# Norm joints: squares ahead of scaled copies, sums of squares inside the dense stream, and products into an unread bank

## The reference

```
block 1, layer l:  u = rms_norm(h, g);  p = u @ w_in            (projection)
                   three mixers (rwkv7, hgrn2, sparse attention) and their gates
                   h = h + (sum of gate * branch) @ w_o          (merge)
                   u = rms_norm(h, g);  h = h + conv_glu(u)      (FFN, width 2816)
                   after layer 1: h = rms_norm(h, g)             (final norm)
block 2, layer l:  h = h + 0.5 * swiglu(rms_norm(h, g))          (FFN)
                   u = rms_norm(h, g);  projection, three mixers, merge
                   h = h + 0.5 * swiglu(rms_norm(h, g))          (FFN)
                   after layer 1: final norm
rms_norm(x, g) = x * rsqrt(mean(x * x over the width) + 1e-6) * g
```

## Time and profile before

| | |
|---|---|
| median of 3 runs | 3233.77 us (3233.0 to 3235.81) |
| the profiled execution | 3229.9 us |
| its span, first to last instruction | 3228.1 us |
| TensorE matmul busy | 2859.5 us, 89% |
| TensorE weight load busy | 2452.1 us, 76% |
| VectorE busy | 1922.0 us, 60% |
| ScalarE busy | 1361.9 us, 42% |
| mean granted TensorE clock | 0.915 of full |

### The profile page before, as it was taken

The page is one execution under the profiler, slowest core; times in us unless marked ns, Lnnn a source line. Parts: engine busy times, 40 slices in busy tenths (PEclk is TensorE's granted clock), DMA queues, the critical chain, the costliest instruction groups (busy, mean ns, idle before and its releaser), DMA issues. The chain is left out here.

```text
span 3228.1 us, 53616 instructions
## 1 busy us (share of the span) xinstructions
PE 2859.5 (89%) x23052; PEld 2452.1 (76%) x23052; DVE 1922.0 (60%) x2576; ACT 1361.9 (42%) x1873; POOL 151.7 (5%) x116
## 2 busy tenths in 40 slices
PE   7898678999897778999998998889999989988899
PEld 6787557888786657888886875678888878756688
DVE  5754766965655766956555444666565644446564
ACT  5413334645413244645453232545454532325443
POOL 0030000000030000000000310000000012000000
PEclk9998888998898888998998998989999988989899
DMA  5211114564111123555542111245645411203453
GB/s 213 92 40 53 66 54 148 197 212 157 66 43 63 66 81 137 202 187 183 198 144 74 40 66 40 93 143 202 220 170 197 141 64 40 72 34 119 138 201 131
DMA packets 54667, 386.18 MB, mean 120 GB/s; under 512 B 6688, under 2 KB 7328, under 8 KB 8352
## 3 DMA queue, kind: packets, MB, share of 16 engines
q1 hardware_dynamic: 54432, 382.76, 34.5%
HBM read 381.69 MB, written 1.05 MB: 119 GB/s over the span
## 5 line engine op out<-in xcount | busy, mean ns | idle before, releaser
L320 PE MATMUL banks<-normed_high,weights_high 128*128 128x256 f16 (+1 forms) x4096 | 1150.7, 281 | 49.6 <-DVE normed_low L414 22.6
L321 PE MATMUL banks<-normed_low,weights_high 128*128 128x256 f16 (+1 forms) x4096 | 1149.7, 281 | 0.0
L322 PE MATMUL banks<-normed_high,weights_low 128*128 128x256 f16 (+1 forms) x4096 | 1148.1, 280 | 0.0
L306 DVE SCALAR_TENSOR_TENSOR weights_low<-weight_ring,weights_high 128x2048 f16<-128x2048 f32 x334 | 761.1, 2279 | 417.2 <-ACT weights_high L300 402.8
L300 ACT ACTIVATE weights_high<-weight_ring 128x2048 f16<-128x2048 f32 x306 | 580.2, 1898 | 299.3 <-PE banks L322 284.0
L320 PE MATMUL banks<-projected,weights_high 128*128 128x256 f16 x1696 | 471.7, 278 | 73.3 <-DVE projected L331 73.3
L320 PEld LDWEIGHTS banks<-normed_high,weights_high 128*128 128x128 f16 (+1 forms) x4096 | 412.8, 101 | 126.3 <-issue 47.3
L321 PE MATMUL banks<-projected,weights_high 128*128 128x256 f16 x1696 | 471.8, 278 | 0.0
L322 PE MATMUL banks<-projected,weights_low 128*128 128x256 f16 x1696 | 471.3, 278 | 0.0
L322 PEld LDWEIGHTS banks<-normed_high,weights_low 128*128 128x128 f16 (+1 forms) x4096 | 411.9, 101 | 59.6
L321 PEld LDWEIGHTS banks<-normed_low,weights_high 128*128 128x128 f16 (+1 forms) x4096 | 411.3, 100 | 59.2 <-issue 1.8
(11 more groups left out here) (390 smaller groups left out, 3251.8 us busy)
## 6 DMA issues: line engine op xcount, KB each, us to landing
weight_ring<-w SPq DMA_DIRECT2D x356, 1024.0 KB, 4.9
small_weights<-small SPq DMA_DIRECT2D x2, 1280.0 KB, 7.9
constants<-const SPq DMA_DIRECT2D x1, 1601.0 KB, 10.1
weight_ring<-w SPq DMA_DIRECT2D x2, 640.0 KB, 3.8
residual<-xt SPq DMA_DIRECT2D x1, 1024.0 KB, 5.0
small_weights<-small SPq DMA_DIRECT2D x2, 512.0 KB, 10.4
out<-residual SPq DMA_DIRECT2D x4, 256.0 KB, 2.8
parameters<-par SPq DMA_DIRECT2D x2, 115.5 KB, 9.6
```

Source lines behind the costliest of these rows:

```text
L306: nc.vector.scalar_tensor_tensor(out=self.part(self.mem.w_low, g), in0=self.part(self.mem.ring, g), scalar=W_SCALE, in1=self.part(self.mem ...
L320: pe.matmul(out, w_high, high, start=start, stop=False, skip_group_check=skip)
L321: pe.matmul(out, w_high, low, start=False, stop=False, skip_group_check=skip)
L322: return pe.matmul(out, w_low, high, start=False, stop=stop, skip_group_check=skip)
```

## The change

- `before_root` gets the next stage's first two weight copies. For an FFN behind a merge (`spaced`) the list is now: table load, squares 0, scaled 0, weight copy, squares 1, scaled 1, weight copy, squares 2, scaled 2, squares 3, root, scaled 3. Elsewhere: table load, both weight copies, squares 0, scaled 0, squares 1, scaled 1, squares 2, squares 3, scaled 2, root, scaled 3.
- The sums are cut into blocks (`sum_two`). In a merge, block 0 stands ahead of tile j=2, block 1 ahead of j=3, block 2 in the middle of j=3. In the last down job block 0 stands ahead of output tile 6. What is not moved stays in `sum`.
- `keep_clock` issues float16 matmuls, 256 columns of a constant tile, into a bank that nobody reads: eight ahead of the last block of sums, four behind it, eight behind the spread.
- `normed`, high and low work in five pieces (1, 1, 2, 2, 2 tiles) instead of four blocks; in the final norms `normed` stays in blocks of two tiles.
- In the FFN stage the low part of the next stage's second job moves from behind residual block 0 to behind block 3.
- In the middle of the program the FFN behind the final norm, and the final norms themselves, use the second order of ScalarE's list. The final norm's TensorE part is as in any norm.

```diff
+def keep_clock(pe, mem, bank, count):
+    still = mem.c("ident").bitcast(F16)
+    for _ in range(count):
+        pe.matmul(mem.ps[:, bank, 0:T], still[:, 0:P], still, start=True, stop=True)
...
+    PIECES = ((0, 1), (1, 1), (2, 2), (4, 2), (6, 2))
...
-    def before_root(self, act, nc):
+    def before_root(self, act, nc, highs, spaced):
+
         nc.scalar.activation(self.unread, self.mem.c("eps", 1), ACT.Sqrt)
+        if not spaced:
+            for high in highs:
+                high(act)
         for b in range(3):
             self.squares(act, nc, b)
-            self.gained(act, nc, b)
+            if b < 2 or spaced:
+                self.gained(act, nc, b)
+            if b < 2 and spaced:
+                highs[b](act)
         self.squares(act, nc, 3)
+        if not spaced:
+            self.gained(act, nc, 2)
         self.root(act, nc)
         self.gained(act, nc, 3)
...
+    def sum_two(self, pe, b):
+
+        assert b == self.summed
+        self.summed += 1
+        pe.wait_ge(self.sig("squares"), b + 1)
+        for k in (2 * b, 2 * b + 1):
             for n in range(NBLK):
                 mm = pe.matmul(self.mem.ps[:, self.sums + n, 0:2], self.u[:, k, n * P:(n + 1) * P],
-                               self.mem.c("ones", 2), start=(k == 0), stop=(k == KT - 1))
-        mm.then_inc(self.sig("square_sums"), 1)
+                               self.mem.c("ones", 2), start=(k == 0), stop=(k == KT - 1),
+                               skip_group_check=True)
+        if b == 3:
+            mm.then_inc(self.sig("square_sums"), 1)
+
+    def sum(self, pe):
+        for b in range(self.summed, 4):
+            if b == 3:
+                keep_clock(pe, self.mem, self.idle_bank, 8)
+            self.sum_two(pe, b)
+        keep_clock(pe, self.mem, self.idle_bank, 4)
 
     def spread(self, pe):
...
         mm.then_inc(self.sig("spread"), 1)
+        keep_clock(pe, self.mem, self.idle_bank, 8)
...
     def scale(self, dve, nc):
+
         self.inverse(dve, nc)
         dve.wait_ge(self.sig("spread"), 1)
-        for b in range(4):
-            self.normed(dve, nc, b, self.u)
-            if b:
-                self.low(dve, nc, b - 1)
-        self.low(dve, nc, 3)
+        last = len(self.PIECES) - 1
+        self.normed(dve, nc, *self.PIECES[0], self.u)
+        for i in range(last):
+            self.normed(dve, nc, *self.PIECES[i + 1], self.u)
+            self.low(dve, nc, i)
+        self.low(dve, nc, last)
...
@@ merge_stage, tensor
             pe.wait_ge(sig("lows"), 6 + j + 1)
+            if j >= 2:
+                following.sum_two(pe, j - 2)
             for n in range(2):
+                if (j, n) == (3, 1):
+                    following.sum_two(pe, 2)
...
@@ ffn_stage, vector
-        next_low(dve, 0)
+        following.low(dve, 0)
...
-            if b == 0:
-                next_low(dve, 1)
+        following.low(dve, 1)
...
@@ ffn_stage, tensor
             for o in range(KT):
+                if i == DOWN - 1 and o == KT - 2:
+                    following.sum_two(pe, 0)
...
-        LOW_SPARE, HIGH_SPARE = (2, 2), (4, 4)
+        LOW_SPARE, HIGH_SPARE = (2, 2, 1), (4, 4, 6)
```

More of the change, by code:

```diff
@@ L341, with __init__ @@
 class Norm:
-    def __init__(self, mem, cut, sig, gain, ready, sums, spread):
+    PIECES = ((0, 1), (1, 1), (2, 2), (4, 2), (6, 2))
+    def __init__(self, mem, cut, sig, gain, ready, sums, spread, idle):
         self.mem, self.sig, self.ready = mem, sig, ready
         self.gain, self.sums, self.spread_bank = CG[gain], sums, spread
+        self.idle_bank, self.summed = idle, 0
         self.u, self.scaled = cut(KT, T), cut(KT, T)
@@ L404, in inverse, with normed, low @@
         nc.vector.reciprocal(self.stat, self.stat).then_inc(self.sig("inverse"), 1)
[L406 to L409, removed]
+    def normed(self, dve, nc, k, n, out):
+        dve.wait_ge(self.sig("gained"), k // 2 + 1)
+        inverse = self.mem.ps[:, self.spread_bank, 0:T].unsqueeze(1).to_broadcast([P, n, T])
+        nc.vector.tensor_tensor(out[:, k:k + n, :], self.scaled[:, k:k + n, :], inverse, ALU.mult
                                 ).then_inc(self.sig("normed"), 1)
[L412 to L416, removed]
+    def low(self, dve, nc, i):
+        k, n = self.PIECES[i]
+        dve.wait_ge(self.sig("u_high"), i + 1)
+        nc.vector.scalar_tensor_tensor(out=flat(self.mem.u_low[:, k:k + n, :]),
+                                       in0=flat(self.u[:, k:k + n, :]), scalar=X_SCALE,
+                                       in1=flat(self.mem.u_high[:, k:k + n, :]), op0=ALU.mult,
                                        op1=ALU.subtract).then_inc(self.sig("u_low"), 1)
@@ L465, in scalar @@
         link, say, need = linker(act, sig, "act_ops")
-        for g in jobs[:2]:
-            stream.high(act, nc, sig, g)
-        norm.before_root(act, nc)
+        norm.before_root(act, nc, [lambda act, g=g: stream.high(act, nc, sig, g)
+                                   for g in jobs[:2]], False)
         norm.highs(act, nc)
@@ L646, in end, with merge_stage @@
         self.out(act, nc, sig, 2 * len(self.jobs) - 1)
-def merge_stage(nc, mem, sig, stream, first, bias, next_low):
+def merge_stage(nc, mem, sig, stream, first, bias, following):
     y_pair = mem.proj[:, 0:3 * MT_, :].bitcast(F16)
@@ L768, in merge_stage, with ffn_stage @@
     return Part(sync, scalar, vector, tensor)
-def ffn_stage(nc, mem, sig, stream, first, gain, ready, spare, conv, factor, loads, next_low):
+def ffn_stage(nc, mem, sig, stream, first, gain, ready, spare, conv, factor, loads, following,
+              spaced=True):
     cut = Cutter(mem.scratch)
@@ L942, in tensor, with final_norm_stage @@
                 mm.then_inc(sig("tiles_done"), 1)
-    return Part(sync, scalar, vector, tensor), early_low, loaded
-def final_norm_stage(nc, mem, sig, gain, ready, spare, next_low, store=None):
+    return Part(sync, scalar, vector, tensor), Early(early_low, norm.sum_two)
+def final_norm_stage(nc, mem, sig, gain, ready, spare, following, store=None):
     norm = Norm(mem, Cutter(mem.scratch), sig, gain, ready, *spare)
@@ L966, in vector @@
         for b in range(4):
-            norm.normed(dve, nc, b, mem.h)
+            norm.normed(dve, nc, 2 * b, 2, mem.h)
             if b % 2:
-                next_low(dve, b // 2)
+                following.low(dve, b // 2)
     def tensor(pe):
@@ L2843, in vector @@
         for n in range(2):
-            low(dve, n)
+            early.low(dve, n)
     def tensor(pe):
```

78 lines of the change are left out of this document (39 added, 39 removed).

## The result

| | before | after |
|---|---|---|
| median of the runs | 3233.64 us (3233.0 to 3235.81, 4 runs) | 3197.15 us (3196.37 to 3202.12, 4 runs) |
| the profiled execution | 3229.9 us | 3197.7 us |
| mean granted clock | 0.915 | 0.932 |

The ratio is 0.989, with a 95% interval of 0.988 to 0.990. The kernel became 36 us faster; 11.2 were forecast and the range went down to 3212 only.

What follows compares the result with a forecast made beforehand. TensorE's dense stream, broken at each of 12 norms, was taken as the bound. Merge joints 5.2, FFN joints 7.6 and others -1.6 gave 11.2 us: 3229.9 to 3218.7, plus 3.9 for the median, say 3222.5; range 3212 to 3238.

Steps and rivals of the forecast that it cites:

- The dense end of a merge joint, +3.25: Merge joints: three moved blocks of sums add 2.74 us and a wait 0.5, so the dense stream ends 3.25 later.
- the wait: Merge joints, ahead of tile j=2: TensorE waits about 0.5 us for the square of residual block 0.
- the rival of a costlier moved block: Dense stream: moved sums and waits cost more, a block 1.3 instead of 0.91 us; 3228 to 3237 us, chance 0.22.
- Sizes with the clock held: Eight merge and FFN joints at full clock: gain 1.8 us per merge joint, 3.2 per FFN joint.
- The pieces, nothing: First group behind a merge joint's norm: cutting the work into pieces gives nothing; whole blocks also take 7.4 us.
- A short half stretch at most FFN joints and at about half of the merge joints: Clock falls briefly at these joints, costing about 0.7 us at a merge joint, 0.8 to 2 at an FFN joint.
- Held: Rival: idle products keep 2.4 GHz at all eight joints, gain 18.4 us, time 3215.4; chance 0.21.
- The others, -1.6: Middle final norm, the end and the first norm: together a loss of 1.6 us.
- The double joint: FFN, final norm, FFN in the middle: 1.5 us lost (0.5 to 2.5), with the FFN's norm at half clock.
- The first norm: First norm: an earlier table load of 1.28 us, but half-clock sums bind; it takes 0.4 us off.
- The end: Final norm at the program's end: 0.5 us lost (0.4 to 1.1).
- My step of adding 3.9 to the forecast: Total: 3218.7 us for the profiled execution raised by 3.9, as the median shown stood above the profile; gives 3222.6.

Runs made afterwards that it cites:

- e6: Changed kernel with VectorE's low part of the last merge job moved behind residual block 0: 3192.11 us, ratio 0.9878.
- e8: Changed kernel with two blocks of sums moved in a merge instead of three, and four idle products instead of eight ahead of the last block: 3199.98 us, 0.9905.
- e7: Changed kernel with normed, high and low in four whole blocks instead of five pieces: 3191.13 us, ratio 0.9874.
- e10: Changed kernel with 14 idle products ahead of the low-rank product of both first-block mixers: 3198.72 us, ratio 0.9893.
- e11: Changed kernel with whole blocks, two moved blocks with four idle products, and 14 idle products ahead of both first-block low-rank products: 3195.09 us, ratio 0.9881.
- e16: Changed kernel with whole blocks and the merge's last low part behind residual block 0: 3190.92 us, ratio 0.9872.
- e13: Kernel before with 8 idle products behind the third group of each of the four projections: 3225.44 us.
- e15: Kernel before with 24 idle products behind the third group of each of the four projections: median 10 us below the kernel before, less the work added.
- e9: Kernel before, unedited, run again for a second profile: 3233.16 us.
- e5: Changed kernel, unedited, run again for a second profile: 3198.62 us, ratio 0.9902.
- e2: Kernel before with only the idle products added, at the same three places of each norm: 3206.3 us, ratio 0.9925.
- e3: Changed kernel with all four blocks of sums back behind the dense stream: 3198.67 us, ratio 0.9899.

## Why the prediction was wrong, step by step

**The dense end of a merge joint, +3.25: right in the sum,** 3.16, and the wait is where it was said to be; but the terms were off both ways and cancelled, which was luck. e6 takes the wait away and gets 0.73 back, where I had 0.50; what is left is 2.43 for three blocks, where I had 2.74. That is 0.81 a block, as at the FFN joints and in e8 (1.62 for two). So the rival of a costlier moved block is dead.

**Sizes with the clock held: right.** Merge joint -1.8 forecast, -1.6 measured; FFN joint -3.2 forecast, -3.5 to -3.8 measured. The root at a merge joint came at 3.16 + 2.54 = 5.7 behind the old dense end, as forecast; that is 1.6 later than before at the last joint and 1.0 to 1.3 at the other three; the first dense product at the same distance from the old dense end (8.5 against 8.1 to 8.7). The spread was not the 0.6 that I took but 0.71, and VectorE's last low part ended 5.5 behind it where I had 5.3. At the FFN joint the idle products on the path cost the 0.8 that I gave them, but the root came 4.2 behind the old dense end where I had 4.56, so 0.6 to 1.0 earlier than before where I had said less than 0.5.

**The pieces, nothing: right** at the eight joints, as the group at 11.33 with and without them shows.

**"A short half stretch at most FFN joints and at about half of the merge joints": wrong.** It cost 4 x 0.5 + 4 x 1.3 = 7.2 in my sum and was nothing: eight joints held, in both profiles of the changed kernel and in those of e6, e7, e8, e10, e11 and e16. I leaned on the earlier trace rows, where eight products of f32 stood in 3.3 us, as the row nearest to the thin sums. It is no measure for 20 full products in 5 us with the sums between them. *Held* was the right rival for the mechanism at the joints; I had given it 0.21, and its time, 3215.4, was still 18 us too high for the reasons that follow.

**"The others, -1.6": wrong in sign,** they are +1.95. The double joint lost 0.2, not 1.5: there the clock was at half for 13.7 us instead of 20.5, where I had taken the half-clock pace of the earlier trace rows as given. The first norm gained 2.4 and not 0.4; the clock rises at 30.9 us instead of 35.2 (in the second profiles 29.0 instead of 33.1), which sets how many products of the first group run at half. This varies between executions: between the two second profiles the gain is 1.5. The end lost about 0.25 for 0.5.

**No term for what is not edited: the largest miss,** 9.7 us. I took the rest of the program as a constant and its falls as fixed. e13 to e15 show that they are not: a delay of 0.87 us is enough to move them. Why the changed kernel's falls came to less rather than more stays open. My reading of e9 against e5, that a joint with a half stretch fixes the distance from which the mixer behind begins and a held joint loosens it, was argued and not tried by itself.

From forecast to measurement, by the profiled executions:

```
forecast gain                      11.2
clock at the eight joints          +7.2
sizes (merge -0.7, FFN +1.4)       +0.7
first, double and last norm        +3.55
outside the joints                 +9.7
sum                                32.35  (measured spans: 3228.1 - 3195.8 = 32.3)
```

The median moved 4 us more than the profile because the profiled execution of before was 3.7 under its median and that of after was on it. My step of adding 3.9 to the forecast was no help: where a profile stands in its runs changes (3.7 and 5.4 us under the median for the kernel before, on it and 3.6 under it for the changed one).

The Trainium skill says in "TensorE: Matmul & The Clock Gate", Part 1, that the gate's timing is not reset by a kernel's start, and that the point at which the clock is released there so differs from run to run. For the first rise the traces agree: 35.2 and 33.1 us in two executions of the kernel before, 30.9 and 29.0 in two of the changed one. Of falls it does not say this. They differed between executions at unedited places (15.07 and 11.75 us for the same code), but not at the eight joints: in the changed kernel they held in both profiles, in the kernel before they fell in both.

## What to carry to other kernels

When TensorE must wait for a short chain on other engines, fill the wait with full-width products into a bank nobody reads, and look at the granted clock of the group behind. Where a run of thin products stood ahead of the filling, it did not prevent the fall at the merge joints (e2, e3); with two of its four blocks inside the dense stream the clock held (e8), at 0.81 us a block. Shorten the chain as well: at all joints together the filling alone gave 16.6 us, the order alone 11.3, all parts together 22.6, and 29.1 with two blocks moved. A kernel whose clock falls at many places is no sum of its stretches: after an edit compare the time at half clock outside the edited stretches before you credit the edit, and do not rank two variants 5 us apart by it.

## What was not expected of the hardware

- Adding 3.5 us of idle products to the dense stream of the projections made the program 7.7 us faster (3225.44 against 3233.16).
- With 14 idle products in a wait of 1.62 us at 791 us the clock stayed at 1.00, where it had fallen in both profiles of the kernel before, and with eight, four and eight of them it stayed through 5 us of sums, root and spread. In the kernel before TensorE was busy for 3.75 of 4 us ahead of a fall, mostly with sums of two columns.
- Between two executions of one program the same low-rank product took 11.75 or 15.07 us.
- What stays open: by what the clock's falls outside the joints come to a total of 396 us in one kernel and 440 in another, and whether a layout can be found on purpose rather than by trial.
